# Nine pre-norm passes through DMA transposes, and the sample tokens' output projections in column groups

## The reference

```python
xn = rmsnorm(x, g_mix_pre); proj = xn @ w_in           # 1024 -> 512 + 3*512
u, bg, cg, h = split(proj)                             # pooling inputs | gated conv
merged = concat(group_rmsnorm(pool_mix(u)), group_rmsnorm(bg * conv3(cg * h)))
x = x + rmsnorm(merged @ w_out, g_mix_post)            # sub-layer 1
x = x + rmsnorm(cross_attn(rmsnorm(x, g_x_pre), mem_k, mem_v, w_q, w_co), g_x_post)
hid = square(relu(rmsnorm(x, g_ff_pre) @ w_up))        # 1024 -> 4096
x = x + rmsnorm(hid @ w_down, g_ff_post)               # sub-layer 3
```

## Time and profile before

| | |
|---|---|
| runs | 915.09, 916.25, 1033.09 us; median 916.25 us |
| the profiled execution | 913.83 us |
| its span, first to last instruction, slowest core (core 3) | 912.3 us |
| spans of the eight cores | 901.6 to 912.3 us |
| granted TensorE clock, mean of a core | 0.990 to 0.993 of full speed |
| PE busy | 858.4 us, 94% of the span |
| DVE, ACT, POOL busy | 396.1, 383.8, 113.4 us |

### The profile page before, as it was taken

One profiled execution on the slowest core, in us unless ns is written; L12 is line 12 of the kernel. 1 busy time (PEld: TensorE's weight loads), 2 busy tenths in 40 slices (PEclk: granted clock), 3 DMA queues, 4 the chain that ended last, 5 costly groups with the idle time before them and its releaser, 6 DMA issues.

```text
span 912.3 us, 13810 instructions; the slowest of 8 cores (901.6 to 912.3 us)
## 1 busy us (share of the span) xinstructions
PE 858.4 (94%) x4708; PEld 407.1 (45%) x4708; DVE 396.1 (43%) x545; ACT 383.8 (42%) x808; POOL 113.4 (12%) x164
## 2 busy tenths in 40 slices
PE   1679998899999999999999999999999999999996
PEld 1334445444445454445445444444444444444442
DVE  4547659566875556546523131323222412222212
ACT  4456647556776565656434031332223410133101
POOL 4363100611520000000012000110001100010000
PEclk9989999999999999999999999999999999999999
DMA  9994054952459629006499962698218981088011
GB/s 236 146 156 64 1 174 149 199 87 44 63 82 174 192 50 241 13 1 93 73 147 145 155 175 70 95 152 129 73 66 145 142 129 47 32 122 124 1 46 47
DMA packets 69801, 97.61 MB, mean 107 GB/s; under 512 B 2618, under 2 KB 60218, under 8 KB 69732
## 3 DMA queue, kind: packets, MB, share of 16 engines
q0 software_dynamic: 58384, 58.85, 46.3%
q1 hardware_dynamic: 11348, 37.87, 12.1%
HBM read 137.50 MB, written 18.07 MB: 171 GB/s over the span
## 4 chain that ended last, share of the span: by engine, by line
PE 85%; DMA 8%; DVE 2%; ACT 2%; issue 1%; SPq 0%; POOL 0%; DVEq 0%; ACTq 0%; POOLq 0%
PE ps L633 83%; PE ps L638 2%; DMA wkv_108<-w_v 2%; DMA win<-w_in 1%; DMA up_129<-w_up 1%; DMA X_63<-xp 1%; DMA x<-X_65 1%; DMA O_58<-mem 1%; DMA X_65<-x 1%; DVE O_58 L669 0%; DVE mg_83 L669 0%; ACT rf_106 L662 0%; SPq L701 0%; ACT sq_104 L662 0%; DVE xT_55 L669 0%
## 5 line engine op out<-in xcount | busy, mean ns | idle before, releaser
L669 DVE TENSOR_TENSOR O_57<-ps,gp 128x1024 f32<-128x1024 f32 (+1 forms) x26 | 31.7, 1221 | 120.0 <-PE ps L633 73.7
L662 ACT ACTIVATE O_57<-ps 128x1024 f32<-128x1024 f32 (+1 forms) x26 | 26.5, 1021 | 125.0 <-PE ps L633 123.6
L669 DVE TENSOR_TENSOR O_58<-ps,gp 128x1024 f32<-128x1024 f32 (+1 forms) x25 | 30.6, 1222 | 96.0 <-PE ps L633 61.9
L662 ACT ACTIVATE rt_128<-ps 128x512 bf16<-128x512 f32 x64 | 38.2, 597 | 72.5 <-PE ps L633 64.5
L662 ACT ACTIVATE rt_127<-ps 128x512 bf16<-128x512 f32 x64 | 38.2, 596 | 70.3 <-PE ps L633 70.3
L633 PE MATMUL ps<-xT_55,win 128*128 128x512 bf16 x256 | 62.8, 395 | 4.6 <-DVE xT_55 L669 2.5
L662 ACT ACTIVATE O_58<-ps 128x1024 f32<-128x1024 f32 (+1 forms) x25 | 25.6, 1023 | 96.0 <-PE ps L633 94.6
L633 PE MATMUL ps<-xT_56,win 128*128 128x512 bf16 x256 | 62.2, 394 | 0.4 <-DVE mg_84 L682 0.4
L633 PE MATMUL ps<-xT_56,up_129 128*128 128x512 bf16 x192 | 42.4, 379 | 0.5 <-DMA up_129<-w_up 0.4
L633 PE MATMUL ps<-xT_55,up_130 128*128 128x512 bf16 x192 | 42.4, 379 | 0.0
L633 PEld LDWEIGHTS ps<-xT_55,win 128*128 128x128 bf16 x256 | 25.1, 101 | 34.9 <-issue 9.3
(11 more groups left out here) (356 smaller groups left out, 1521.4 us busy)
## 6 DMA issues: line engine op xcount, KB each, us to landing
up_129<-w_up POOLq DMA_DIRECT2D x11, 1024.0 KB, 11.4
up_130<-w_up POOLq DMA_DIRECT2D x11, 1024.0 KB, 12.3
up_131<-w_up POOLq DMA_DIRECT2D x10, 1024.0 KB, 10.8
win<-w_in POOLq DMA_DIRECT2D x4, 768.0 KB, 27.7
wout<-w_out POOLq DMA_DIRECT2D x1, 2048.0 KB, 46.2
wq<-w_q POOLq DMA_DIRECT2D x1, 2048.0 KB, 16.5
wco<-w_co POOLq DMA_DIRECT2D x1, 2048.0 KB, 16.3
X_61<-xp SPq DMA_DIRECT2D x2, 512.0 KB, 6.4
```

Of the source, the lines that this page charges most:

```text
L662: return e.activation(out=L(out), in_=L(in_), func=func, scale=scale, **kw)
L669: opts.append(("dve", lambda e, L: e.tensor_tensor(out=L(out), in0=L(in0), in1=L(in1), op=op), c_dve(n, per)))
```

## The change

Nine of the twelve passes (tile 3 of the mixing, all of attention and of the MLP) go through `pre_tile_dma`: ACT and DVE make `xs` as before, then SP issues one DMA transpose of the piece from `xs` straight into `xT`, and when all four pieces have landed DVE multiplies `xT` in place by the gain, in eight instructions of 512 columns. The first three passes stay on PE. In the attention loop the pass now stands ahead of the four heads instead of behind the second.

The sample residual is kept as `Xs`, 128 partitions by 256 columns: partition group b (32 partitions) holds channels 256b to 256b+255 of the 32 tokens. `out_smp` puts each group's result on its own 32 partitions of PSUM, so that four matmuls with the same 32 stationary columns, each moving 256 columns of the weight, go to four different column groups of the array. The sum of squares over a token is then folded over the four groups by a small matmul with `fold4` (`rstd_s`), and the sample's pre-norm for attention and MLP takes two transposes instead of eight (`pre_smp`). `share=3` is a cost given to the scheduler. The host lays `x_sample`, the gains and the output out to match.

```diff
+    def pre_tile_dma(t, gc, buf):
+        for i in range(NSUB):
+            X = Xof[(t, i)][:, :]
+            ss = stat(128)
+            xs = xsr[xs_n[0] % 2][:, :]
+            xs_n[0] += 1
+            act(xs, X, AF.Square, accum=ss)
+            rs = rstd(ss, 128)
+            ts(xs, X, rs, ALU.mult)
+            dst = r3(buf[:, :], 8)[:, :, i * 128:(i + 1) * 128]
+            P.add([("sp", lambda e, L, dst=dst, xs=xs: e.dma_start_transpose(out=dst, in_=xs), 0.06)],
+                  reads=[xs], writes=[dst], nbytes=262144)
+        for c in range(8):
+            v = buf[:, c * TN:(c + 1) * TN]
+            ts(v, v, gcs[:, gc * 8 + c:gc * 8 + c + 1], ALU.mult, per=0.25)
...
+    def rstd_s(ss):
+        ps = PS(1, reserve=0)
+        mm(ps.v(0, 128, 0, 1), f4[:, :], ss, True, True)
...
+    def out_smp(chunks, nk, w):
+        ps = PS(1)
+        for kc in range(nk):
+            for b in range(4):
+                mm(ps.v(32 * b, 32 * b + 32, 0, 256), chunks(kc), w(kc, b // 2)[:, (b % 2) * 256:(b % 2 + 1) * 256],
+                   kc == 0, kc == nk - 1, share=3)
+        full = ps.v(0, 128, 0, 256)
+        ss = stat(128)
+        Ob = Or[o_n[0] % 2][:, 0:256]
+        o_n[0] += 1
+        act(Ob, full, AF.Square, accum=ss)
+        tt(Ob, full, gps[:, :], ALU.mult)
+        rs = rstd_s(ss)
+        stt(Xs[:, :], Ob, rs, Xs[:, :], ALU.mult, ALU.add)
...
             if cc == 1 and t + 1 < NT:
-                pre_tile(t + 1, 0, xT[(t + 1) % 2])
+                pre_tile_dma(t + 1, 0, xT[(t + 1) % 2])
             elif cc == 1:
-                pre_tile(2, 1, xT[0])
+                pre_tile_dma(2, 1, xT[0])
...
+        if p < 3:
+            pre_tile_dma((3, 0, 1)[p], 1, xT[(p + 1) % 2])
+        else:
+            pre_smp(2)
+            pre_tile_dma(0, 2, xT[0])
         fins = []
         for hh in range(4):
             step(attn_head(p, hh))
-            if hh == 1 and p < 3:
-                pre_tile((3, 0, 1)[p], 1, xT[(p + 1) % 2])
-            elif hh == 1:
-                pre_sub(Xe[0:NS, :], NS, 2, r3(xTe[:, :], 8)[:, :, 0:NS])
-                pre_tile(0, 2, xT[0])
...
         if t + 1 < NT:
-            pre_tile(t + 1, 2, xT[(t + 1) % 2])
+            pre_tile_dma(t + 1, 2, xT[(t + 1) % 2])
```

More of the change, by code:

```diff
@@ L527, in build_program @@
     invc = din("invc", [128, 64]); pvec = din("pvec", [128, 24]); ident = din("ident", [128, 128])
+    xs4 = din("xs4", [128, 256]); gs4 = din("gs4", [3, 128, 256]); fold4 = din("fold4", [128, 128])
     gnames = ["g_mix_post", "g_x_post", "g_ff_post"]
@@ L536, in build_program @@
     wpool_d = din("w_pool", [128, 512])
-    yp = dout("yp", [TP, D]); ysm = dout("ysm", [NS, D])
+    yp = dout("yp", [TP, D]); ysm = dout("ysm", [128, 256])
     o_pool_p = dout("pool_p", [16, 512]); o_conv_p = dout("conv_p", [2, 512])
@@ L569, in build_program @@
     Xr = [fix("X%d" % i, D) for i in range(8)]
-    Xe = fix("Xe", D); xTe = fix("xTe", 8 * NX, BF16)
+    Xs = fix("Xs", 256); gps = fix("gps", 256); f4 = fix("f4", 128)
+    Xe = Or[1]; xTe = fix("xTe", 8 * NX, BF16)
     mgs = fix("mgs", 8 * NS, BF16); hids = fix("hids", 32 * NS, BF16)
@@ L628, in build_program, with mm @@
     psum = {F32: psum_f, BF16: [p.bitcast(BF16) for p in psum_f]}
-    def mm(out, lhsT, rhs, start, stop, cost=None):
-        n = ncols(rhs)
+    def mm(out, lhsT, rhs, start, stop, share=1):
+        n = ncols(rhs) / share
         P.add([("pe", lambda e, L: e.matmul(L(out), lhsT=lhsT, rhs=rhs, start=start, stop=stop,
@@ L728, in build_program @@
     load(Xe[0:NX, :], xe[:, :], NX * 4096)
+    load(f4[:, :], fold4[:, :], 65536, lead=LEAD // 2)
+    load(Xs[:, :], xs4[:, :], 131072, lead=LEAD // 2)
     load(idf[:, :], ident[:, :], 65536)
@@ L819, in out_tile, with load_gps, pre_smp @@
             dma("sp", dst[row:row + 128, :], X, 524288, wr=(dst is not yp))
-    def out_smp(chunks, nk, w, gp):
-        ps = PS(2)
-        for h in range(2):
-            for kc in range(nk):
-                mm(ps.v(0, NS, h * 512, (h + 1) * 512), chunks(kc), w(kc, h), kc == 0, kc == nk - 1)
-        post(ps, Xe[0:NS, :], NS, gp)
+    def rstd_s(ss):
+        ps = PS(1, reserve=0)
+        mm(ps.v(0, 128, 0, 1), f4[:, :], ss, True, True)
+        a = stat(128)
+        b = stat(128)
+        act(a, ps.v(0, 128, 0, 1), AF.Ln, scale=1.0 / D, bias=epsb[:, 0:1])
+        act(b, a, AF.Exp, scale=-0.5)
+        return b
+    def load_gps(k):
+        load(gps[:, :], gs4[k], 131072, lead=LEAD // 2)
+    def out_smp(chunks, nk, w):
[12 more added lines that the diff above has]
+        stt(Xs[:, :], Ob, rs, Xs[:, :], ALU.mult, ALU.add)
+    def pre_smp(gc):
+        ss = stat(128)
+        xs = xsr[xs_n[0] % 2][:, 0:256]
+        xs_n[0] += 1
+        act(xs, Xs[:, :], AF.Square, accum=ss)
+        rs = rstd_s(ss)
+        ts(xs, Xs[:, :], rs, ALU.mult)
+        ps = PS(1, reserve=1)
+        for h in range(2):
+            tr(ps.v(0, 128, h * 128, (h + 1) * 128, BF16), xs[:, h * 128:(h + 1) * 128], idb[:, :])
+        for h in range(2):
+            cv3 = lambda a: a.rearrange("p (b t) -> p b t", b=4)
+            src = ps.v(0, 128, h * 128, (h + 1) * 128, BF16, cv3)
+            dst = xTe[:, :].rearrange("p (b h t) -> p b h t", b=4, h=2)[:, :, h, 0:NS]
+            gb = gcs[:, gc * 8:(gc + 1) * 8].rearrange("p (b h) -> p b h", h=2)[:, :, h].unsqueeze(2).to_broadcast([128, 4, NS])
+            tt(dst, src, gb, ALU.mult)
     wi = lambda c, kc: win[:, c * 1024 + kc * 128: c * 1024 + (kc + 1) * 128]
@@ L1217, in build_program @@
     load_gp("g_mix_post")
+    load_gps(0)
     for k in range(2):
@@ L1253, in build_program @@
     kv_mem()
-    out_smp(lambda kc: mgs[:, kc * NS:(kc + 1) * NS], 8, wo, gslot["g_mix_post"])
+    out_smp(lambda kc: mgs[:, kc * NS:(kc + 1) * NS], 8, wo)
     pre_tile(2, 0, xT[0])
@@ L1278, in build_program @@
     load_gp("g_x_post")
-    pre_sub(Xe[0:NS, :], NS, 1, r3(xTe[:, :], 8)[:, :, 0:NS])
+    load_gps(1)
+    pre_smp(1)
     for p, t in enumerate((2, 3, 0, 1)):
@@ L1306, in build_program @@
         if p == 1:
-            out_smp(lambda kc: mgs[:, kc * NS:(kc + 1) * NS], 8, wc, gslot["g_x_post"])
+            out_smp(lambda kc: mgs[:, kc * NS:(kc + 1) * NS], 8, wc)
     load_gp("g_ff_post")
+    load_gps(2)
     ups = None
@@ L1325, in build_program @@
         if t + 1 < NT:
-            pre_tile(t + 1, 2, xT[(t + 1) % 2])
+            pre_tile_dma(t + 1, 2, xT[(t + 1) % 2])
         out_tile(t, hid, 32, wd, gslot["g_ff_post"], yp)
         if t == 0:
-            out_smp(lambda kc: hids[:, kc * NS:(kc + 1) * NS], 32, wd, gslot["g_ff_post"])
-            dma("sp", ysm[:, :], Xe[0:NS, :], NS * 4096, wr=False)
+            out_smp(lambda kc: hids[:, kc * NS:(kc + 1) * NS], 32, wd)
+            dma("sp", ysm[:, :], Xs[:, :], NS * 4096, wr=False)
         if t + 2 < NT:
@@ L1390 @@
     inv_mid = np.stack([np.full(16, 1.0 / w) for w in (2, 4, 8, 16)]).astype(np.float32)
+    quad = lambda a: f(np.asarray(a).reshape(32, 4, 256).transpose(1, 0, 2)).reshape(128, 256)
+    shared["fold4"] = f(np.tile(np.eye(32, dtype=np.float32), (4, 4)))
+    shared["gs4"] = f(np.stack([np.repeat(f(g).reshape(4, 256), 32, axis=0) for g in (g_mix_post, g_x_post, g_ff_post)]))
     in_maps = []
@@ L1401 @@
         d["xe"] = np.concatenate([f(x_sample[2 * c:2 * c + 2]).reshape(32, D), halo], axis=0)
+        d["xs4"] = quad(f(x_sample[2 * c:2 * c + 2]).reshape(32, D))
         sp = np.zeros((2, 16, 512), np.float32)
@@ L1423 @@
         yp[b, half * TP:(half + 1) * TP] = r["yp"]
-        ys[2 * c:2 * c + 2] = r["ysm"].reshape(2, 16, D)
+        ys[2 * c:2 * c + 2] = r["ysm"].reshape(4, 32, 256).transpose(1, 0, 2).reshape(2, 16, D)
         if half == 1:
```

## The result

The changed kernel takes 966.06 us (median of 4 runs, 963.9 to 972.83) against 916.01 us before: a ratio of 1.056 (95% interval 1.049 to 1.063). 895 us was predicted, with a range that ended at 940. Now and then an execution of any of these kernels runs on one or both dies at a lower clock and takes longer; the ratios leave such executions out, the medians count them.

What follows compares the result with a forecast made beforehand. PE was taken to bound the kernel after startup: 913.8 us, less 16.2 for transposes and 10.1 for sample projections, plus 6 for waits, gives 893.5; with 1.8 for undisturbed runs, 895 us, range 882 to 940.

Steps and rivals of the forecast that it cites:

- I take L = 5 us: All DMA transposes: time from issue to landing, taken as 5 us; waits then lose 6 us in all.
- The sum: Whole kernel: 913.8 less 16.2 and 10.1, plus 6 lost in waits; above a landing time L of 7, losses are 12L - 62.
- the packing: Sample's projections: 192 matmuls in different column groups at 0.056 us each, 10.8 us in place of 20.9.
- Nothing below L = 14 in the MLP: MLP passes: no loss for landings under 14 us, the result being wanted only after 56 us of `w_down` matmuls.
- The attention's mechanism: Attention's second tile: two `xs` buffers delay ACT's square, DVE's scalings wait before the heads' outputs; PE loses 2 us.
- The slower rival: Mixing, attention, MLP: small packets make waits on DVE and ACT the bound; 940 us at 9.4 us landing, chance 0.20.
- its 9.4 us: Landing of a transpose in 256-byte packets: 1024 over 16 engines, 7.4 us, with the floor of 2.0.
- SP's issue at nothing: SP's queue: issuing the 36 transposes, and the loads queued behind them, was costed at nothing.
- The sample projections: Sample's projections: 96 matmuls of 512 columns replaced by 192 of 256, saving 10.1 us.
- The rival without overlap: Sample's projections: column groups do not overlap, 22.8 us in place of 10.8, so 907 us; chance 0.08.
- the 953 us worked out from it: Whole kernel: eight blocks transposed one after the other, 10.5 us at the skill's DMA price, give about 953 us.
- The 16.2 us of PE's transposes: Nine pre-norm passes: 288 transposes of 0.056 us leave PE, saving 16.2 us of span.

Runs made afterwards that it cites:

- the three MLP passes alone: Kernel before with the sample's column groups, and DMA transposes only in the three MLP passes inside the tile loop, other passes on TensorE: 906.74 us, ratio 0.994.
- the run of small copies: Changed kernel with each DMA transpose replaced by a plain DMA of the same 256 KB in 1024 pieces of 256 bytes, untransposed: 959.08 us, ratio 1.046.
- the column groups alone: Changed kernel with all twelve pre-norm passes back on TensorE at their old places, only the sample's new path kept: 897.98 us, ratio 0.982.
- the run with four `xs` and few loads: Changed kernel with four `xs` buffers instead of two, and each MLP weight load moving one block in eight: 898.08 us, ratio 0.985.

## Why the prediction was wrong

- **The step that failed is "I take L = 5 us", one length for all 36 transposes.** With nothing of POOL's queue beside them they land in 3.0 to 5.7 us, most under 3.6; beside its loads in 5.0 to 20.7 us, most over 13. The sum was linear in one L, so it could not see that a few late landings make the loss. The landings read for L were all of SP's own transfers; which loads POOL would have in flight at the nine places stood in no term. With the MLP's loads cut and the pair gone the ratio is 0.985, near the forecast's 895 / 916.25 = 0.977, and in part by luck: the sum had the packing 5.3 us too dear.
- **"Nothing below L = 14 in the MLP"** was the second step to fail. It asked when the result is wanted, not what is queued behind the wait. The products `hid` are, and PE stood 15.91 us at a landing of 20.7; the three MLP passes alone, whose longest landing of 13.9 is below 14, cost 11 us.
- **The attention's mechanism was right**: ACT held by the pair, DVE by the scaling in front of the heads; a run without either gives back about half of the loss. The slower rival (0.20) had it, with packets of 256 bytes (248 measured). But it too used one L for all passes, and its 9.4 us priced the packets alone, where an undisturbed transpose takes 3.0; the landings at the bad places are up to 20.7, and the time is past its 940.
- **SP's issue at nothing** was wrong as a fact (up to 10.15 us for one transpose) and nearly harmless: the run of small copies, at a median issue of 0.6 us, loses all but 0.010 of it.
- **The sample projections** were taken at 10.8 us for 192 matmuls, with 6.3 as the lower bound. The block of 128 takes 3.68, so 192 take 5.5: 15.4 us saved, not 10.1. By the Trainium skill, TensorE: Matmul & The Clock Gate, Part 3, three column tiles give 2.38; four gave 3.8 here. The rival without overlap fell.
- The upper end of the forecast's own range, 903 us, is 905.5 by its own terms (14 us lost at L = 6, 7.9 saved with a packing of 13 us); nothing hung on it.
- By the Trainium skill, VectorE: DVE Perf Modes (Rules for kernel authors), TensorE is to be used for a transpose of 128x128 where PSUM will do. The advice holds for this kernel as it is loaded; the page's price of 1309 ns per block by DMA (The three transpose paths) does not describe it, since eight blocks land in 3.0 us undisturbed. That the 953 us worked out from it came near the result is luck: the loss came from a few late landings, not from one long L.

**The 16.2 us of PE's transposes** did go. PE's busy time in the column groups alone, and in the run with four `xs` and few loads:

```profile
PE 844.7 (94%) x4802; PEld 403.7 (45%) x4802; DVE 391.4 (44%) x548; ACT 380.1 (42%) x807; POOL 114.2 (13%) x164
...
PE 828.7 (93%) x4514; PEld 388.2 (43%) x4514; DVE 371.5 (41%) x590; ACT 375.6 (42%) x801; POOL 98.9 (11%) x164
```

That is 16.0 less, and yet the time is the same within the intervals (0.985 and 0.982): waits took it, so at no place did it show as a gain. In the changed kernel PE is busy 839.8, 11 us more than in the second line for the same matmuls, at a mean clock of 0.950 where that run has 0.985: PE comes out of a long wait at the lower level, as at 518. The clock had no term in the sum.

## What to carry to other kernels

In this kernel a transfer's length depended on its neighbours: before pricing a DMA that something waits for, list what the other queues move in the same microseconds, and count packets as well as bytes. A result that is wanted late is not hidden if the instruction that waits for it stands in a queue of fixed order in front of work that is wanted now; price what is behind it. Where the plan is made beforehand, a wait whose length varies lost either way here, early or late, and work on an engine that is full but punctual can be the cheaper one.

## What the runs showed that was not expected

- Four column groups of 32 partitions, each with 256 columns and its own weight load, pass at 3.68 us / 128 = 0.029 us per matmul, 0.115 for four: what one matmul of 256 columns took alone before (0.119).
- SP's issue of a DMA transpose takes 1.23 us undisturbed, that of a plain copy of the same 256 KB 0.47 us in 128 rows and 0.60 us in 1024 pieces. Beside weight loads the issue of a transpose stretches to 10.15 us, that of the pieces only to 1.01.
- Eight scalings of 128x512 bf16 in place take 2.18 us together, 0.27 each, below the 0.425 of a two-input product.
